# A two-phase FFN: up-projection in pairs of seven half products, all down blocks behind it, split squares kept in DRAM

## The chip, the cores and the metric

One core of a Trainium2 chip runs the whole kernel: three layers of a network on 1024 tokens, float32 throughout, one launch. The metric is device time in microseconds (us); each time given for the kernel before comes from three runs of it or from one profiled execution. The engines are named as in the profile: PE (TensorE matmul), DVE (VectorE), ACT (ScalarE), POOL (GpSimd), SP (SyncE, which issues DMAs).

## The reference, cut to what is touched

```
m = rmsnorm(h, g_mlp[i])                                             # [1024 tokens, 1024]
h = h + jnp.square(jax.nn.relu(m @ w_up[i])) @ w_down[i]             # 1024 -> 4096 -> 1024
gate = jax.nn.sigmoid(rmsnorm(h, g_ple[i]) @ w_ple_gate[i])
h = h + gate * (p[i] @ w_ple_proj[i])
return rmsnorm(h, g_final)
```

Everything ahead of these lines (a recurrent and latent-attention layer, a state-space layer, a convolution and attention layer) is the same in both kernels. The change concerns the second line, called the FFN below.

## The kernel before, in words

Float32 products run on PE as three matmuls: each operand is split into a high part (rounded to the PE's float32r) and a low part (what is left), and hi·hi, lo·hi and hi·lo are added in PSUM. One matmul takes 128 rows of weights and 512 tokens. Making a low part is a subtraction on DVE or POOL; making a high part is a copy on ACT or POOL.

Weights come as slabs of 512 KB. SP fetches them in the order of use into the two slots of `w_stage` (`fetch`, L614), each when the slab two earlier has been split (`s_w_ready`). POOL splits them into a ring of eight entries of `w_hi` and `w_lo`; an entry holds two 128-row tiles (`entry_hi` L707, `entry_lo` L711), and is free when PE has used it.

The order of the FFN is the list `FFN_ORDER`. A block is 512 of the 4096 hidden columns and has four up slabs (`up`, L1459) and four down slabs (`down`, L1485). Up slabs of block b+1 stand between the up and the down slabs of block b, so that while PE works on one kind, the other engines prepare the other. An up slab is 48 matmuls: 8 row tiles, 2 token halves, 3 parts. DVE then takes the relu and the root out of PSUM (`up_tile`, L2973), ACT squares it (L2176), and `upper_split` and `lower_split` (L2980 to L3001) with their ACT copies (L2184 to L2194) make what the down slabs read.

Seven of the eight down blocks use seven products of half size where a plain 2 x 2 product of quarters has eight (the list `SEVEN`, in the form that keeps sums of sums). Quarters of the weights are added on DVE (`weight_sums`, L3010 to L3015), quarters of the squares in the splits; each product goes to a half bank of PSUM, and DVE adds it where it belongs (`down_added`, L3032). A down slab is so 42 matmuls, not 48. The last block is plain (`last_down`, L1507).

## Time and profile before

| | us |
|---|---|
| median of 3 runs (2645.07 to 2648.64) | 2646.43 |
| the profiled execution, first to last instruction | 2643.2 |
| first matmul of the FFN (L1459) | 1876.5 |
| first matmul of the plain last block (L1507) | 2492.9 |
| PE busy over the span | 2572.9 (97%) |
| DVE, ACT, POOL busy over the span | 1599.2, 1001.6, 1140.9 |

The profile has one execution. Its busy PE counts a matmul from its start to its modelled end, and matmuls overlap, so the spacing of their starts is what they cost. A low busy share of DVE or POOL over the span says little of a stretch: rows further down are from stretches of the FFN alone. The profile gives no duration of the execution outside its first and last instruction; the median of the runs is 3.2 us above that span.

### The profile page before, as it was taken

What the parts mean: (1) busy time and instruction counts of PE and PEld (TensorE: products, weight loads), DVE (VectorE), ACT (ScalarE), POOL (GpSimd) and SP (SyncE); (2) the same over time, 40 slices, a digit from 0 to 9 for tenths busy, and PEclk for the clock granted to TensorE, in tenths of its full rate; (3) what the DMA queues carried; (4) which work ended last, traced back from release to release, by engine and by line L of the source; (5) the groups of instructions that cost most, each with busy time, mean ns of one, the idle gap of its engine ahead of it and who ended that gap; (6) DMA issues with size and microseconds to landing.
All of it is one profiled execution on the core that took longest, in us unless ns stands there. A gap on an engine that the chain in (4) does not pass through costs nothing.

```text
span 2643.2 us, 33209 instructions
## 1 busy us (share of the span) xinstructions
PE 2572.9 (97%) x12880; PEld 2055.9 (78%) x12880; DVE 1599.2 (61%) x1936; ACT 1001.6 (38%) x1434; POOL 1140.9 (43%) x1422
## 2 busy tenths in 40 slices
PE   8999999999999999999999999999999999999998
PEld 6877878687787787877776777767888888888886
DVE  6636663777647648557776455564455565555556
ACT  3527881436405315225365445563201111111132
POOL 4633344532432432432442222214565557655653
PEclk9999999999999999999999999999999999999999
DMA  3110002212112112111230010003111111111312
GB/s 139 48 51 27 24 25 90 86 59 100 52 55 73 58 49 71 66 59 66 90 112 24 25 33 25 33 17 104 56 49 48 48 56 56 54 43 49 120 47 80
DMA packets 44822, 156.36 MB, mean 59 GB/s; under 512 B 4928, under 2 KB 5312, under 8 KB 44672
## 3 DMA queue, kind: packets, MB, share of 16 engines
q1 hardware_dynamic: 31392, 110.11, 12.8%
q10 hardware_dynamic: 13280, 44.17, 4.6%
q8 instruction: 103, 1.69, 0.3%
q14 instruction: 47, 0.39, 0.0%
HBM read 141.55 MB, written 12.71 MB: 58 GB/s over the span
## 4 chain that ended last, share of the span: by engine, by line
PE 85%; DVE 8%; ACT 4%; issue 2%; POOL 1%; ACTq 0%; DVEq 0%; POOLq 0%
PE PS L784 38%; PE PS L1459 13%; PE PS L1485 10%; PE PS L1114 4%; PE PS L1021 3%; PE PS L1507 2%; PE PS L1347 1%; PE PS L920 1%; PE PS L1330 1%; PE PS L1147 1%; PE PS L1157 1%; PE PS L1151 1%; PE PS L934 1%; PE PS L1370 1%; DVE mla_neg_max L2397 1%
## 5 line engine op out<-in xcount | busy, mean ns | idle before, releaser
L637 POOL CAST w_hi<-w_stage 128x1024 fp32r<-128x1024 f32 x130 | 145.0, 1115 | 1048.4 <-PE PS L784 758.2
L640 POOL TENSOR_TENSOR w_lo<-w_stage,w_hi 128x256 fp32r<-128x256 f32 x520 | 492.9, 979 | 10.4
L784 PE MATMUL PS<-XH,w_hi 128*128 128x512 f32 x1216 | 386.7, 399 | 9.0 <-ACT ssd_z L1899 3.3
L784 PE MATMUL PS<-XL,w_hi 128*128 128x512 f32 x1216 | 375.9, 390 | 0.0
L784 PE MATMUL PS<-XH,w_lo 128*128 128x512 f32 x1216 | 375.4, 390 | 0.0
L784 PEld LDWEIGHTS PS<-XH,w_hi 128*128 128x128 f32 x1216 | 221.5, 188 | 65.4 <-issue 12.9
L784 PEld LDWEIGHTS PS<-XH,w_lo 128*128 128x128 f32 x1216 | 228.3, 188 | 48.7
L784 PEld LDWEIGHTS PS<-XL,w_hi 128*128 128x128 f32 x1216 | 228.3, 188 | 48.6
L711 POOL TENSOR_TENSOR w_lo<-w_stage,w_hi 128x256 fp32r<-128x256 f32 x260 | 220.1, 853 | 0.0
L707 POOL CAST w_hi<-w_stage 128x256 fp32r<-128x256 f32 x260 | 125.7, 486 | 185.6 <-PE PS L1459 108.2
L1459 PE MATMUL PS<-raw_hi,w_hi 128*128 128x512 f32 x512 | 158.2, 390 | 0.0
L1459 PE MATMUL PS<-raw_hi,w_lo 128*128 128x512 f32 x512 | 157.8, 389 | 0.0
L1459 PE MATMUL PS<-raw_lo,w_hi 128*128 128x512 f32 x512 | 157.7, 389 | 0.0
L1485 PE MATMUL PS<-ffn_u_hi,w_hi 128*128 128x512 f32 x392 | 152.6, 389 | 0.0
L1485 PE MATMUL PS<-ffn_u_hi,w_lo 128*128 128x512 f32 x392 | 152.6, 389 | 0.0
L1485 PE MATMUL PS<-ffn_u_lo,w_hi 128*128 128x512 f32 x392 | 152.6, 389 | 0.0
L3032 DVE TENSOR_TENSOR H<-H,PS 128x512 f32<-128x512 f32 x140 | 96.1, 686 | 76.9 <-PE PS L1485 76.9
L2973 DVE SCALAR_TENSOR_TENSOR ffn_t<-PS,root 128x1024 f32<-128x1024 f32 x32 | 39.2, 1225 | 154.2 <-PE PS L1459 145.0
L2176 ACT ACTIVATE ffn_t<-ffn_t 128x1024 f32<-128x1024 f32 x32 | 34.0, 1061 | 240.1 <-DVE ffn_t L2973 240.1
L1459 PEld LDWEIGHTS PS<-raw_hi,w_hi 128*128 128x128 f32 x512 | 96.1, 188 | 20.3 <-issue 0.5
L1459 PEld LDWEIGHTS PS<-raw_lo,w_hi 128*128 128x128 f32 x512 | 96.1, 188 | 19.9
L1459 PEld LDWEIGHTS PS<-raw_hi,w_lo 128*128 128x128 f32 x512 | 96.1, 188 | 19.9
(459 smaller groups left out, 5421.5 us busy)
## 6 DMA issues: line engine op xcount, KB each, us to landing
w_stage<-w SPq DMA_DIRECT2D x202, 512.0 KB, 3.4
ssd_sum_rows<-sums_kept ACTq DMA_DIRECT2D x32, 512.0 KB, 3.7
H<-x_t ACTq DMA_DIRECT2D x8, 512.0 KB, 8.3
pj_kept<-ple_proj_tiles ACTq DMA_DIRECT2D x8, 512.0 KB, 2.6
h_kept<-H ACTq DMA_DIRECT2D x8, 512.0 KB, 3.0
H<-h_kept ACTq DMA_DIRECT2D x4, 1024.0 KB, 5.5
out_t<-out_tiles SPq DMA_DIRECT2D x16, 256.0 KB, 2.1
x_again<-x_t ACTq DMA_DIRECT2D x12, 256.0 KB, 3.1
```

The source lines that it names most:

```text
L637: nc.gpsimd.tensor_copy(w_hi[:, slot, :, :], w_stage[:, slot, :, :]).then_inc(s_w_hi, 1)
L640: nc.gpsimd.tensor_tensor(w_lo[:, slot, k:k + 2, :], w_stage[:, slot, k:k + 2, :], w_hi[:, slot, k:k + 2, :].bitcast(F32), ALU.subtract).t ...
L707: nc.gpsimd.tensor_copy(ring(w_hi, e), src).then_inc(s_eh.sem, 1)
L711: nc.gpsimd.tensor_tensor(ring(w_lo, e), src, ring(w_hi, e).bitcast(F32), ALU.subtract).then_inc(done, count)
L784: mm = nc.tensor.matmul(outs[:, half, :], wt[:, slot, k, :], a[:, k - first, half * HB:(half + 1) * HB], start=(k == whole[0] and wt is w_ ...
L1021: mm = nc.tensor.matmul(PS[:, 2 * (n % 2) + half, :], wt[:, n % 2, k, :], a[:, k, half_cols(half)], start=(k == 0 and wt is w_hi and a is ...
L1114: mm = nc.tensor.matmul(PS[:, half, :], wt[:, n % 2, k, :], a[:, k, half * HB:(half + 1) * HB], start=(k == 0 and wt is w_hi and a is XH), ...
L1459: mm = nc.tensor.matmul(PS[:, 2 * (c % 2) + half, :], ring(wt, e + k // 2, k % 2), a[:, k, half * HB:(half + 1) * HB], start=(k == 0 and w ...
L1485: mm = nc.tensor.matmul(PS[:, BANK[j], :], ring(wt, e + i, k), a[:, ACTS_AT[j], k, :], start=(j not in BEFORE and k == 0 and wt is w_hi an ...
L1507: mm = nc.tensor.matmul(PS[:, 4 + 2 * e + half, :], ring(wt, e0 + k // 2, k % 2), a[:, t, half * HB:(half + 1) * HB], start=(first and wt ...
L2973: v.scalar_tensor_tensor(out=FT[:, c % 2, :], in0=flat(c % 2), scalar=0.0, in1=RSQ[:, :], op0=ALU.max, op1=ALU.mult).then_inc(s_ue, 1)
L3032: v.tensor_tensor(dst, dst, src, ALU.add).then_inc(s_dr, 1)
```

## The change

Up slabs are taken in pairs. Two pairs stay plain; for the other 14, a pair (1024 rows by 256 hidden columns by 1024 tokens) becomes seven products of quarters, each of 4 row tiles by 512 tokens by 3 parts, 12 matmuls. Sums of the token quarters are made once, before the phase (`token_sums`, `sums_lo`). Sums of weight quarters are made for each pair: three on DVE (`pair_sums`), one on POOL (`pair_difference`). ACT makes the high parts of all weights from here on (`pair_hi`, `down_hi`), POOL the low parts (`pair_part`, `down_part`).

All up pairs run first, then all down blocks. The split squares no longer stay in SBUF: for each pair seven pieces (four in the last two pairs), each 128 x 2 x 512 float32, are made in one of a few `U_PLACE`s, stored to DRAM by SP (`store`), and loaded again before their down block (`load`: four DMAs a block, of two pieces of both pairs each, the last of one).

The diff, cut to its core:

```diff
-FFN_ORDER = [("up", 0, 0), ("up", 0, 2), ("up", 0, 1), ("up", 0, 3)]
-for _b in range(1, FFN_BLOCKS):
-    FFN_ORDER += ([("up", _b, 0), ("up", _b, 2)] + [("down", _b - 1, _s) for _s in range(4)]
-                  + [("up", _b, 1), ("up", _b, 3)])
+PAIRS, PLAIN_PAIRS, DOWN_BLOCKS = 2 * FFN_BLOCKS, 2, FFN_BLOCKS - 1
+FFN_ORDER = [("up", _p // 2, _q) for _p in range(PAIRS) for _q in (_p % 2, _p % 2 + 2)]
+FFN_ORDER += [("down", _b, _s) for _b in range(DOWN_BLOCKS) for _s in range(4)]
 FFN_ORDER += [("last", FFN_BLOCKS - 1, _s) for _s in range(4)]
...
+            def next_slab(n):
+                sp.wait_ge(s_w_ready, 4 * (n - 1))
+                fetch(n, n % 2)
...
+            for p in range(PLAIN_PAIRS + 1, PAIRS):
+                stores(p - 2, slice(0, 2))
+                next_slab(pair_slab(p))
+                stores(p - 2, slice(2, 7))
+                next_slab(pair_slab(p) + 1)
+            p = PAIRS - 1
+            stores(p - 1, slice(0, 2))
+            next_slab(d0)
...
+            load(0, 0)
+            stores(p - 1, slice(2, 4))
...
+            load(0, 3)
+            next_slab(d0 + 1)
...
+            load(0, 1)
...
+            load(0, 2)
+            stores(p, slice(0, 2))
+            next_slab(d0 + 2)
+            stores(p, slice(2, 4))
...
+            for group in range(4):
+                load(1, group)
+            next_slab(d0 + 3)
+            for b in range(DOWN_BLOCKS - 1):
+                next_slab(d0 + 4 * b + 4)
+                next_slab(d0 + 4 * b + 5)
+                if b + 2 < DOWN_BLOCKS:
...
+                    for group in range(4):
+                        load(b + 2, group)
...
+                next_slab(d0 + 4 * b + 6)
+                next_slab(d0 + 4 * b + 7)
...
+            def up_pair(p):
+                for i, j in enumerate(SEVEN):
+                    if i in (4, 6):
+                        pe.wait_ge(s_w_ready, 4 * (n + 1 + (i == 6)))
+                    else:
+                        s_pd.wait(pe, 5 * turn + i + 1 - (i > 4))
...
+                    elif j in BEFORE:
+                        pe.wait_ge(s_ue, up_read({3: "c22", 4: "u3"}[j], p))
...
+                    for k in range(4):
+                        for wt, hl in ((w_hi, 0), (w_hi, 1), (w_lo, 0)):
+                            mm = nc.tensor.matmul(PS[:, 4 * (p % 2) + BANK[j], :], ring(wt, e + 2 * i + k // 2, k % 2), up_acts(j, hl, k),
...
+            for p in range(PLAIN_PAIRS, PAIRS):
+                if p > PLAIN_PAIRS:
+                    square_quad(p - 1, "f21")
+                u_hi(QUADS[p - 1][2], p - 1)
+                first_copied(p)
+                pair_hi(p, 4)
+                for j in QUADS[p - 1][3:]:
+                    u_hi(j, p - 1)
+                pair_hi(p, 5)
+                pair_hi(p, 6)
...
+            def pair_sums(p):
+                n, turn = pair_slab(p), p - PLAIN_PAIRS
+                a11, a12, a21, a22 = (w_stage[:, m, 4 * h:4 * h + 4, :] for m in range(2) for h in range(2))
+                for slot in range(2):
+                    dve.wait_ge(s_w_loaded[slot], 16 * (n // 2) + 16)
...
+                v.tensor_tensor(WS2[:, 0, :, :], a21, a22, ALU.add).then_inc(s_ws, 1)
+                dve.wait_ge(s_ws, 3 * turn + 1)
+                v.tensor_tensor(WS2[:, 1, :, :], WS2[:, 0, :, :], a11, ALU.subtract).then_inc(s_ws, 1)
...
+            for p in range(PLAIN_PAIRS, PAIRS):
+                u3(p)
+                c22(p)
+                f(3, p)
+                f(1, p)
+                if p + 1 < PAIRS:
+                    pair_sums(p + 1)
+                else:
+                    weight_sums(0, 0)
+                c12(p)
+                f(8, p)
+                u_steps(p, p + 1 if p + 1 < PAIRS else None)
```

On DVE `u_steps` makes the low parts of pieces 1 and 3, the last PSUM sum `c21` and its relu, the differences of pieces 5, 7, 6 and 4, and the other low parts. `SEVEN` is 1, 6, 5, 7, 2, 3, 4; of a pair's weights, products 1, 2 and 4 take a quarter as loaded, 6, 5 and 3 take DVE's sums, 7 takes POOL's difference. The second slab of a pair holds two of the quarters that the first sum adds.

Three places show the order that this makes.

SP before, from the program's start to its end (`w_stage` are the weight slots; the branch rows are the loop over slabs):

```order
L614 DMA w_stage_49<-w 128x1024 x2
L620 UNCONDITIONAL_BRANCH
L620 ISA
L614 ISA
L614 DMA w_stage_49<-w 128x1024
L614 ISA
L614 DMA w_stage_49<-w 128x1024
L620 REGISTER_ALU
L620 COMPARE_AND_BRANCH
L628 DMA out_t<-out_tiles_165 128x512 x16
```

SP after, between two second slabs of pairs in the middle of the up phase (the first and last row are such fetches; `ffn_u_place0` to `4` are the places of split squares, `u_kept` is in DRAM):

```order
L715 DMA w_stage_49<-w 128x1024
L737 DMA u_kept<-ffn_u_place0_161 128x1024
L737 DMA u_kept<-ffn_u_place1_162 128x1024
L715 DMA w_stage_49<-w 128x1024
L737 DMA u_kept<-ffn_u_place2_163 128x1024
L737 DMA u_kept<-ffn_u_place3_164 128x1024
L737 DMA u_kept<-ffn_u_place0_161 128x1024
L737 DMA u_kept<-ffn_u_place4_165 128x1024
L737 DMA u_kept<-ffn_u_place1_162 128x1024
L715 DMA w_stage_49<-w 128x1024
```

Before, only weights stood in this queue until the outputs. Now two stores stand ahead of the first slab's fetch of each pair, and five between it and the second slab's.

DVE before, from one up tile to the first PSUM add of the down slabs:

```order
L2973 SCALAR_TENSOR_TENSOR ffn_t<-PS,root 128x1024
L3010 TENSOR_TENSOR w_sums<-w_stage 128x256
L3012 TENSOR_TENSOR w_sums<-w_sums,w_stage 128x256
L3013 TENSOR_TENSOR w_sums<-w_stage 128x256
L3015 TENSOR_TENSOR w_sums<-w_stage,w_sums 128x256
L2973 SCALAR_TENSOR_TENSOR ffn_t<-PS,root 128x1024
L3032 TENSOR_TENSOR ffn_shared<-ffn_shared,PS 128x512
```

DVE after, from the weight sums of the next pair to the first difference (`up_w_sums` are those sums, `up_partial` the running sum of products, `ffn_t` the quarters that become squares):

```order
L3421 TENSOR_TENSOR up_w_sums<-w_stage 128x512
L3423 TENSOR_TENSOR up_w_sums<-up_w_sums,w_stage 128x512
L3425 TENSOR_TENSOR up_w_sums<-w_stage,up_w_sums 128x512
L3367 TENSOR_TENSOR ffn_t<-up_partial,PS 128x512
L3381 SCALAR_TENSOR_TENSOR ffn_t<-ffn_t,root 128x512
L3409 TENSOR_TENSOR ffn_u_place_165<-ffn_t,ffn_u_place_165 128x512
L3409 TENSOR_TENSOR ffn_u_place_161<-ffn_t,ffn_u_place_161 128x512
L3371 TENSOR_TENSOR ffn_t<-up_partial,PS 128x512
L3381 SCALAR_TENSOR_TENSOR ffn_t<-ffn_t,root 128x512
L3402 TENSOR_TENSOR ffn_u_place_162<-ffn_t 128x512
```

Before, the weight sums belonged to down slabs alone. Now the three sums of the next pair stand ahead of the rest of this pair's evacuation and split.

SP after, at the turn from the up phase to the down phase (`u_last_kept` takes the pieces of the plain last block, `ffn_u_even` and `ffn_u_odd` are the loaded pieces of even and odd blocks; the weight fetches are the second, the third, and the fourth to sixth down slab):

```order
L764 DMA ffn_u_even_last_172<-u_kept 128x2048
L715 DMA w_stage_49<-w 128x1024
L764 DMA ffn_u_even_171<-u_kept 128x2x2048 x2
L737 DMA u_last_kept<-ffn_u_place0_161 128x1024
L737 DMA u_last_kept<-ffn_u_place1_162 128x1024
L715 DMA w_stage_49<-w 128x1024
L737 DMA u_last_kept<-ffn_u_place2_163 128x1024
L737 DMA u_last_kept<-ffn_u_place3_164 128x1024
L764 DMA ffn_u_odd_173<-u_kept 128x2x2048 x3
L764 DMA ffn_u_odd_173<-u_kept 128x2048
L715 DMA w_stage_49<-w 128x1024 x3
```

Before, the squares of the first down block were already in SBUF when its slabs came. Now seven megabytes a block stand in the same queue as the weights, the second block's ahead of the fourth down slab.

## Rows read from the trace of the kernel before

**Rows 1.** The chain that ended last, from the FFN on: start, length, what.
```profile
1943.67 38.08 PE PS L1485 x168
1981.75 43.52 PE PS L1459 x192
...
2471.34 21.76 PE PS L1459 x96
2493.11 10.88 PE PS L1507 x48
```

**Rows 2.** Busy time of the engines in the blocks, then PE clock, DMA share, GB/s.
```profile
1943.50:2470.70 527.20, 527.20 (x2327) 436.68 (x2326) 300.23 (x436) 72.79 (x85) 335.98 (x583) 1.00 0.17 53
```

**Rows 3.** Timeline of DVE, a split right behind a down block: start, length, instruction.
```profile
2144.98 0.69 DVE L3032 TENSOR_TENSOR H<-H,PS 128x512 f32<-128x512 f32 x1 [0.67 <-PE PS L1485]
2145.59 1.07 DVE L2980 TENSOR_TENSOR ffn_u_sums<-ffn_t 128x512 f32<-128x512 f32 x1
...
2153.60 0.88 DVE L3001 TENSOR_TENSOR ffn_u_lo<-ffn_u_sums,ffn_u_hi 128x512 fp32r<-128x512 f32 x1
```

**Rows 4.** Timeline of DVE, the lower half of a later split.
```profile
2169.09 0.69 DVE L2989 TENSOR_TENSOR ffn_u_sums<-ffn_t 128x512 f32<-128x512 f32 x1 [1.13 <-ACT ffn_t L2176]
...
2173.50 0.68 DVE L3001 TENSOR_TENSOR ffn_u_lo<-ffn_u_sums,ffn_u_hi 128x512 fp32r<-128x512 f32 x1
```

**Rows 5.** Timeline of POOL, inside the stretch of rows 3.
```profile
2150.89 1.71 POOL L711 TENSOR_TENSOR w_lo<-w_stage,w_hi 128x256 fp32r<-128x256 f32 x1
```

**Rows 6.** Groups of instructions by form, FFN blocks alone: busy us, mean ns.
```profile
L711 POOL TENSOR_TENSOR w_lo<-w_stage,w_hi 128x256 fp32r<-128x256 f32 x183 | 149.7, 824 | 0.0
...
L711 POOL TENSOR_TENSOR w_lo<-w_sums,w_hi 128x256 fp32r<-128x256 f32 x108 | 79.6, 737 | 0.0
...
L3015 DVE TENSOR_TENSOR w_sums<-w_stage,w_sums 128x256 f32<-128x256 f32 x27 | 16.7, 620 | 0.0
...
L3012 DVE TENSOR_TENSOR w_sums<-w_sums,w_stage 128x256 f32<-128x256 f32 x27 | 11.5, 425 | 0.9
...
L2184 ACT ACTIVATE ffn_u_hi<-ffn_t 128x512 fp32r<-128x512 f32 x12 | 7.6, 634 | 215.1 <-PE PS L1485 214.6
```

**Rows 7.** The same view of the whole span, one group of POOL.
```profile
L654 POOL TENSOR_TENSOR mla_q_lo<-mla_q,mla_q_hi 128x1024 fp32r<-128x1024 f32 x8 | 19.0, 2378 | 78.7 <-ACT mla_q_hi L1664 78.7
```

**Rows 8.** DMA issues: KB each, median us from issue to landing.
```profile
w_stage<-w SPq DMA_DIRECT2D x202, 512.0 KB, 3.4
...
pj_kept<-ple_proj_tiles ACTq DMA_DIRECT2D x8, 512.0 KB, 2.6
```

**Rows 9.** Timeline of ACT, copies that wait for 512 KB loads issued in a row.
```profile
13.57 1.06 ACT L1580 ACTIVATE XH<-H 128x1024 fp32r<-128x1024 f32 x1 [0.54 <-DMA H<-x_t]
14.85 1.06 ACT L1580 ACTIVATE XH<-H 128x1024 fp32r<-128x1024 f32 x1 [0.22 <-DMA H<-x_t]
16.12 1.06 ACT L1580 ACTIVATE XH<-H 128x1024 fp32r<-128x1024 f32 x1 [0.22 <-DMA H<-x_t]
```

**Rows 10.** Busy time while two loads of 2 MB ran; the last two columns are DMA.
```profile
2475.00:2477.00 2.00, 2.00 (x10) 1.65 (x9) 2.00 (x4) 0.00 (x0) 0.83 (x2) 1.00 1.00 410
...
2479.00:2481.00 2.00, 2.00 (x11) 1.65 (x10) 0.99 (x2) 0.00 (x0) 1.37 (x2) 1.00 1.04 420
```

More of the change, by code:

```diff
@@ L199, with pair_slab, _uses @@
 FFN_ORDER += [("last", FFN_BLOCKS - 1, _s) for _s in range(4)]
 FFN_AT = {_key: N_FFN + _n for _n, _key in enumerate(FFN_ORDER)}
+def pair_slab(p):
+    return N_FFN + 2 * p
 RING = 8
-ENTRY, ENTRY_OWNER, FREED = {}, [], {}
+ENTRY, USED, FREED = {}, [], {}
 _freed = 0
-for _key in FFN_ORDER:
-    if _key[0] == "last":
-        break
-    _n, _size = FFN_AT[_key], 4 if _key[0] == "up" else 7
-    ENTRY[_n], FREED[_n] = len(ENTRY_OWNER), _freed
-    ENTRY_OWNER += [(_n, _i if _i < _size - 1 else None) for _i in range(_size)]
-    _freed += _size - 1
+def _uses(n, parts, slabs, wide):
+    global _freed
+    ENTRY[n], FREED[n] = len(USED), _freed
+    for _i in range(parts):
+        if _i in slabs:
+            USED.extend([("slab", slabs[_i])] * wide)
+        else:
+            _freed += 1
+            USED.extend([("part", _freed)] * wide)
@@ new lines, in stores, with stored, used @@
+            def stores(p, part):
+                for j in [j for j, q in LOWS if q == p][part]:
+                    store(j, p)
+            def stored(p):
+                n = sum(len(QUADS[q]) for q in range(p))
+                for r in range(U_PLACES):
+                    if PLACE_ORDER[:n].count(r):
+                        s_us[r].wait(sp, 16 * PLACE_ORDER[:n].count(r))
+            def used(token):
+                if token[0] == "slab":
+                    sp.wait_ge(s_slab, token[1])
+                else:
+                    s_we.wait(sp, token[1])
@@ new lines, in load @@
+            def load(b, group):
+                first, last = 2 * group, min(2 * group + 2, 7)
+                if b >= 2:
+                    n = FFN_AT["down", b - 2, 3]
+                    used(USED[ENTRY[n] + last - 1])
+                if b % 2:
+                    dst = U_ODD[:, first:last, :, :, :]
+                else:
+                    dst = U_EVEN[:, first:last, :, :, :] if group < 3 else U_EVEN4[:, :, :, :].unsqueeze(1)
+                sp.dma_start(dst.rearrange("p q i l t -> p q (i l t)").bitcast(F32),
+                             u_kept[b, first:last, :, :, :, :].rearrange("q p i l t -> p q (i l t)")).then_inc(s_ur[b % 2][group].sem, 16)
@@ L624, in _ @@
+            for n in range(N_PLE - 4, NSLAB):
+                next_slab(n)
             for half in range(2):
@@ L753, in program @@
+            for d in range(4 * DOWN_BLOCKS):
+                for i in range(7):
+                    down_part(d, i)
+            for turn, n in enumerate(range(N_PLE - 4, NSLAB)):
+                plain_slab(n, 2 * PLAIN_PAIRS + turn)
         class Tiles:
@@ new lines, in first_copied, with used @@
+            def first_copied(p):
+                turn = p - PLAIN_PAIRS
+                kind, count = pair_use(p, 0)
+                s_we.wait(act, count)
+                if turn:
+                    act.wait_ge(s_ue, up_read("c21", p - 1))
+                nc.scalar.activation(U2[:, :], PS[:, 4 * (p % 2) + BANK[1], :], ACT.Copy).then_inc(s_p1.sem, 1)
+            def used(token):
+                kind, count = token
+                if kind == "slab":
+                    act.wait_ge(s_slab, count)
+                else:
+                    s_we.wait(act, count)
@@ new lines, in ring, with pair_hi @@
+            def ring(t, e, wide=1):
+                return t[:, :, :, :].rearrange("p a b c -> p (a b) c")[:, e % RING * 2:e % RING * 2 + 2 * wide, :]
+            def pair_hi(p, i):
+                j, n = SEVEN[i], pair_slab(p)
+                e, turn = ENTRY[n] + 2 * i, p - PLAIN_PAIRS
+                used(USED[e + 1 - RING])
+                if j in PAIR_RAW:
+                    slot, k = PAIR_RAW[j]
+                    act.wait_ge(s_w_loaded[slot], 16 * (n // 2) + 16)
+                    src = w_stage[:, slot, k:k + 4, :]
+                else:
+                    if j == 7:
+                        s_w3.wait(act, turn + 1)
+                    else:
+                        act.wait_ge(s_ws, 3 * turn + {5: 1, 6: 2, 3: 3}[j])
+                    src = WS2[:, SUM_AT[j], :, :]
+                nc.scalar.activation(ring(w_hi, e, 2), src, ACT.Copy).then_inc(s_ah.sem, 1)
```

736 lines of the change are left out of this document (499 added, 237 removed).

## The prediction

> **What bounds the kernel now.** I read the chain of waits in order of time first, from the FFN on. It is PE and nothing else: 38.08 us for the 168 matmuls of four down slabs, 43.52 us for the 192 of four up slabs, in turn, without a wait between [rows 1]. Both give 0.2267 us per matmul. Then the busy times of that stretch [rows 2]: PE is busy for all of its 527.2 us at a granted clock of 1.00 (the 2.4 GHz level), DVE for 57% of it, POOL for 64%, ACT for 14%, and DMA for a 0.17 share. So a matmul that is taken away here shortens the kernel by 0.2267 us, as long as the other engines and the queue keep up. The other three views say how much they have left: timelines of DVE and POOL where both work at once [rows 3 to 5], groups by form [rows 6, 7], and the DMA views [rows 8 to 10].
>
> **What is removed.** A plain pair is 96 matmuls, 21.76 us; seven half products are 84, 19.04 us. Over 14 pairs that is 168 matmuls, **-38.1 us**. The down slabs (42) and the plain last block keep theirs. A half product is 12 matmuls, 2.72 us in an up pair and 1.36 us in a down slab.
>
> **What must fit under 19.04 us.** ACT gets 19 operations of 128 x 512 a pair at 0.63 us [rows 6], 12 us: it fits. POOL gets seven low parts and a difference of 128 x 512. No row has that form; between 0.737 us for 256 columns and 2.378 us for 1024 [rows 6, 7] it is 1.28 us alone, 10.3 us a pair. DVE gets 23 operations. Behind a down block nine splits of 11 times 512 columns took from 2145.59 to 2154.48 us [rows 3], 0.81 us per 512 columns, with POOL at work beside them (a low part took 1.71 us there [rows 5], against 0.74 alone); with POOL mostly waiting, eight took from 2169.09 to 2174.18 us [rows 4], 0.64 us. DVE reads PSUM beside POOL undisturbed: 0.61 us from start to start [rows 3]. So 17 operations with two SBUF operands and 6 with one from PSUM take 14.5 to 17.4 us. Each engine fits by itself. What doesn't is a loop through all of them and the queue.
>
> **The loop.** Per pair SP now issues two weight fetches and seven stores of 512 KB. Nine transfers at 1.27 us, the spacing at which loads issued in a row landed (14.85 to 16.12 [rows 9]), are 11.4 us, also what 410 to 420 GB/s make of them [rows 10]. It is their order that counts. Say the second slab of pair p+1 has landed at W.
> - DVE runs in order: three weight sums, two evacuation steps, two low parts, two more steps, the first difference of pair p. Eight have two SBUF operands (0.81 us; POOL has its difference and three low parts to do meanwhile), two read PSUM (0.61 us): 7.7 us.
> - ACT copies the difference, then the first product out of PSUM, then makes the high part of pair p+1's fifth product: 3 x 0.63 = 1.9 us. It can't take the last of these first, since it stands behind the copy that waits.
> - POOL makes that product's low part: 1.4 us (1.28 with the 824 to 737 ns of rows 6). Only this frees the slot for the next pair's first slab.
> - SP fetches it: 3.4 us to landing [rows 8]. Five stores of pair p and the second slab's fetch follow: 6 x 1.27 = 7.6 us, since their pieces are ready (DVE makes them within 6.5 us of the difference) before their turn in the queue.
> - Five hand-overs of 0.04 us, as between dependent operations of one engine: 0.2 us.
>
> That is W of the next pair: **22.2 us**, more than 19.04 and more than 21.76. From below: DVE at 0.64 us throughout, POOL at 1.28, is 20.7 us. From above: if POOL's four operations (5.1 us) each held DVE up in full, 26 us. I take 22.2, for the stretch of rows 3 is the nearest, and keep 20.7 to 24.5 for the range.
>
> PE sees it as a wait for the second product (sums, high part, low part: W + 3.8 us). Pair 3's second slab comes by the same steps some 20 us into pair 2, which costs 2.5 us. Twelve turns from pair 3 to pair 15 cost 12 x (22.2 - 19.04) = 37.9 us. **Up phase: -38.1 + 2.5 + 37.9 = +2.3 us.** The time saved in matmuls is waited for again.
>
> **The turn to the down phase.** A load of two pieces is 2 MB, 5.1 us of the queue. Count from W of pair 15. Its last matmul ends at 3.8 + 6 x 2.72 = 20.1. The first down slab's fetch goes out at 11.0 (the loop's steps, with a square on ACT in place of DVE's difference) and lands at 14.4; behind it stand 2 MB (19.5), two stores (22.0), 1 MB (24.6), a slab (25.8), 2 MB (30.9), 2 MB (36.0). PE wants the third product's pieces at 22.8 and gets them at 30.9 (8.1 us), the fifth's at 33.6 and gets them at 36.0 (2.4 us). The fourth down slab is fetched behind four stores, a slab and the 7 MB of the second block: 36.0 + 6.4 + 17.8 + 1.2 = 61.4. DVE's sums for it stand in order ahead of the third slab's adds, and PE's sixth product there, due at 56.4, waits for one: 61.4 + 1.9 (sums, 425 and 620 ns [rows 6]) + 1.2 = 64.5, 8.1 us. **+18.6 us**, between 10 (fetches that partly pass the loads) and 25.
>
> **Each later block.** The loads for the block after next start when the last slab's second product is done, 2.7 us into it; 2.1 us later data flows, 17.8 us long, then the third slab of the next block: 24.1 us, 14.5 into that block. DVE stands at its sums from 11.7 and adds again from 16.4; PE's sixth product is due at 16.3 and starts at 17.6: 1.3 us, five times, **+6.5 us**, from 0 to 12.
>
> **Nothing elsewhere.** Token sums (16 DVE operations, about 11 us, before the first evacuation) hide behind two plain slabs; PSUM is used twice as deep; the tail keeps its order.
>
> Sum: 2.3 + 18.6 + 6.5 = +27.4 us on the profiled span of 2643.2 us. The median of the runs is 3.2 us above that; 2646.4 + 27.4 = **2674 us**.
>
> **The rivals.**
> - *The second slab doesn't wait for the stores: faster.* If its fetch overtook them (the rows show a full queue in order for loads, and nothing of stores beside loads), the loop would be 22.2 - 5 x 1.27 = 15.9 us, and PE would set the pace at 19.04. Left are 12 us at the turn and 3 behind it: -38.1 + 15 = -23 us, 2623 us. The point that decides is 19.04 us a pair. For it: a lone store lands in 2.6 us [rows 8], and DMA was at 0.17 [rows 2]. Against: 1.27 us at 1.00 share is all that the queue gave. Chance 0.2.
> - *DVE and POOL in each other's way.* With the loop at 24.5 to 26 us: 12 x 5.5 to 7 = 66 to 84 us, so 2702 to 2720 us. For it: 1.71 us against 0.74 [rows 5]. Against: DVE's own 0.81 was only a quarter above 0.64. Chance 0.1. The Trainium skill (SBUF — State Buffer, "Who interferes with whom") has it that a DVE operation with two SBUF inputs and a POOL operation that reads SBUF exclude each other for a whole instruction. By that the loop would be the 26 us. Rows 3 and 5 agree as to POOL and bear out only part of it for DVE.
> - *All of it even.* The loop at its low bound (1.7 x 12 = 20 us) and the turn at 10, with 5 behind: -38.1 + 2.5 + 35 = about -1 us, 2646 us. Chance 0.1.
>
> **How the numbers follow.** The forecast has 0.6. The low ends of its terms (2.5 + 20 + 10 + 0 - 38.1) give -6, the high ends (2.5 + 65.5 + 22 + 10 - 38.1) +62. From 2630 to 2712 us leaves out most of the first rival and the top of the second, about 2 in 10. A change of 0.2% (5.3 us) is about what runs of this kernel can tell from none. Faster: the first rival and a little of the forecast's low end, 0.22. Same: the even case, 0.1. Slower: 0.68.
>
> **What would show it.** PE waiting at the second product of most pairs, for POOL's low part, that for DVE's sums, that for the fetch of `w_stage`; starts of up pairs 22 us apart; fetches with a median far over 3.4 us to landing, and the second slab landing behind stores; one or two waits of 8 us in the first down block and its fourth slab. It is wrong if pairs start 19.04 us apart, or if PE waits at the sixth product, for the PSUM sums on DVE, rather than at the second. If stores go out while a fetch issued later lands first, the first rival holds.

## The result, and the profile after

The changed kernel takes 2752.09 us (median of 4 runs, 2747.81 to 2755.55), the kernel before, beside it, 2645.75 us (2645.03 to 2648.64): a ratio of 1.0398, 95% interval 1.0383 to 1.0413. The forecast had the direction right and the size wrong: +27 us was forecast, +106 us came, outside the range. The profiled execution spans 2752.3 us.

The busy times of the up pairs and of the down blocks, with the columns of [rows 2] (length; PE, PEld, DVE, ACT, POOL; PE clock, DMA share, GB/s):

```profile
1924.90:2283.70 358.80, 301.36 (x1176) 238.43 (x1176) 295.46 (x321) 152.30 (x270) 176.13 (x114) 0.91 0.50 184
2285.80:2602.30 316.50, 284.43 (x1176) 231.46 (x1177) 179.41 (x305) 77.11 (x193) 148.38 (x205) 0.93 0.60 235
```

In [rows 2] PE was busy for the whole stretch at a clock of 1.00. Now it is 361.8 us from the last plain matmul (1921.9) to the end of the 14 pairs (2283.7), where plain ones took 14 x 21.76 = 304.6: **+57.2 us** (forecast +2.3). From there to the end of the split down blocks it is 318.6 us, where seven blocks of [rows 1] took 266.6: **+52.0 us** (forecast 18.6 + 6.5 = +25.1). Together that is 109.2 us, the difference of the two profiled spans (2752.3 and 2643.2): the rest of the kernel is as before. Each of the two stretches has 1176 matmuls, 266.6 us at 0.2267. The windows above leave out 3.0 and 2.0 us of waiting ahead of them; with these PE idles for 60.4 us in the up phase and 34.1 in the down blocks, and its own work is 34.8 and 17.8 us longer than it would be at full clock.

What PE waits for there (waits of PE; us in total, times, longest):

```profile
PE PS L1700 <- DVE ffn_t L3363: 53.1, 13, 4.2
PE PS L1723 <- POOL w_lo L944: 27.5, 8, 8.6
PE PS L1723 <- DMA ffn_u_even<-u_kept: 6.6, 1, 6.6
...
PE PS L1700 <- DVE ffn_t L3309: 3.4, 1, 3.4
```

L3363 is the second PSUM sum of a pair, so PE waits at the sixth product, once a pair, for 4.2 us: the sign that the forecast named for being wrong. The pace, from DVE's first weight sum of each pair (view of one line: duration min/median/max in ns, first and last start):

```profile
L3421 DVE TENSOR_TENSOR up_w_sums<-w_stage x12: 691/693/694, 1951.1 to 2235.6; 128x512 f32<-128x512 f32 x12
```

Eleven pairs in 284.5 us: **25.9 us a pair**, where 22.2 was forecast and a plain pair took 21.76. The chain of waits through one such pair, then POOL and DVE near its end:

```profile
2003.07 0.70 DVE up_w_sums L3421
...
2003.79 1.67 DVE up_w_sums L3423
...
2008.10 3.40 DVE ffn_u_place L3409 x2
...
2018.27 4.04 DVE ffn_u_place L3409 x3
...
2022.33 0.32 SPq L737
...
2022.70 2.33 DMA w_stage<-w
2025.02 3.54 issue
2028.56 0.70 DVE up_w_sums L3421
```

```profile
2020.05 3.38 POOL L932 TENSOR_TENSOR w_lo<-w_stage,w_hi 128x512 fp32r<-128x512 f32 x2
...
2028.61 1.78 POOL L917 TENSOR_TENSOR up_w_sums<-w_stage 128x512 f32<-128x512 f32 x1 [5.18 <-DMA w_stage<-w]
```

```profile
2022.23 0.68 DVE L3358 TENSOR_TENSOR ffn_t<-up_partial,PS 128x512 f32<-128x512 f32 x1
```

It is a loop, and a loop through the second slab's fetch, as forecast; but it closes elsewhere. DVE works from the sums to its last low part of a square piece (2003.07 to 2022.3: 19.2 us); SP, in order, issues the last store (L737) and only then the fetch, at 2022.70. The slab has landed 5.8 us later, behind the stores: POOL, which does nothing else then, waits for it until 2028.5. The place that this slab goes to had come free only at 2021.7, with the seventh product's low part, the first of the two at 2020.05. The DVE instructions themselves are long. Their groups by form from 1950 to 2200 us (busy us, mean ns), then one of POOL's:

```profile
L3409 DVE TENSOR_TENSOR ffn_u_place<-ffn_u_place 128x512 fp32r<-128x512 f32 x39 | 46.3, 1205 | 0.0
L3409 DVE TENSOR_TENSOR ffn_u_place<-ffn_t,ffn_u_place 128x512 fp32r<-128x512 f32 x30 | 41.6, 1411 | 0.0
...
L3402 DVE TENSOR_TENSOR ffn_u_place<-ffn_t,ffn_u_place 128x512 f32<-128x512 f32 x10 | 17.5, 1750 | 0.2 <-DMA u_kept<-ffn_u_place 0.2
L3423 DVE TENSOR_TENSOR up_w_sums<-up_w_sums,w_stage 128x512 f32<-128x512 f32 x10 | 16.6, 1663 | 0.3
...
L3425 DVE TENSOR_TENSOR up_w_sums<-w_stage,up_w_sums 128x512 f32<-128x512 f32 x10 | 6.9, 692 | 0.3
```

```profile
L917 POOL TENSOR_TENSOR up_w_sums<-w_stage 128x512 f32<-128x512 f32 x10 | 17.9, 1788 | 55.0 <-DMA w_stage<-w 55.0
```

The same form on DVE takes 692 ns (L3425) or 1663 ns (L3423). The sum that is long, L3423, is the one beside which POOL makes the pair's difference (L917). L3358, which adds a PSUM bank to one operand in SBUF, takes 0.68 us although POOL makes a low part at the same time (the rows of 2020.05 and 2022.23).

In the down blocks, the third slab of a block, followed in the one case (timelines of SP, DVE and PE):

```profile
2383.33 7.13 SPq L764 DMA_DIRECT2D ffn_u_odd<-u_kept  x4
2390.50 9.48 SPq L715 DMA_DIRECT2D w_stage<-w  x2
```

```profile
2404.72 0.42 DVE L3437 TENSOR_TENSOR w_sums<-w_stage 128x256 f32<-128x256 f32 x1 [3.01 <-DMA w_stage<-w]
...
2405.52 0.96 DVE L3440 TENSOR_TENSOR w_sums<-w_stage 128x256 f32<-128x256 f32 x1
...
2407.87 2.06 DVE L3459 TENSOR_TENSOR H<-H,PS 128x512 f32<-128x512 f32 x3
```

```profile
2285.82 1.08 PE L1723 MATMUL PS<-ffn_u_even,w_hi 128*128 128x512 f32 x2 [2.01 <-POOL w_lo L944]
...
2408.69 1.07 PE L1723 MATMUL PS<-ffn_u_even,w_hi 128*128 128x512 f32 x2 [2.27 <-POOL w_lo L944]
```

The fetch goes out behind four loads, lands 14.2 us later, DVE stands for 3.0 us, and PE waits 2.27 us (the row of PE ahead of that one is the first wait of the turn). The profile names POOL's low part, but the sixth product, at which PE stands here, also waits for DVE's add of the third, the first of the three at 2407.87: it ended 0.1 us before PE went on, and the low parts of this slab had been made by 2399.6. The DMA issues, to [rows 8]:

```profile
w_stage<-w SPq DMA_DIRECT2D x202, 512.0 KB, 3.4
```

Over the whole kernel the fetches' median is the 3.4 us it was, where the forecast expected far more: what is late is shown by the single fetches above, not by the median. The clock, in three windows from one wait of the up phase on (columns as above):

```profile
2019.70:2023.80 4.10, 0.00 (x0) 0.00 (x0) 3.96 (x5) 0.63 (x1) 3.73 (x3) 0.92 1.04 422
2023.84:2029.95 6.11, 6.11 (x14) 4.75 (x15) 2.54 (x4) 2.38 (x4) 1.34 (x1) 0.50 0.62 245
2030.20:2045.00 14.80, 14.80 (x67) 12.23 (x66) 14.01 (x17) 7.78 (x14) 7.22 (x6) 1.00 0.28 92
```

PE does nothing for 4.1 us, and the next 14 matmuls take 6.11 us at a granted clock of 0.50, the 1.2 GHz level, in place of 3.2; then it is at 1.00 again.

### The profile page after: what moved, and what is told of

The parts are those of the page before. It is cut to its first block, busy times and chain, and to the rows that moved or that the text cites. A ratio compares the mean times of both kernels' runs of the same rounds, so it can differ in the third digit from the quotient of the medians.

```text
span 2752.3 us, 33519 instructions
## 1 busy us (share of the span) xinstructions
PE 2587.9 (94%) x12712; PEld 2052.3 (75%) x12712; DVE 1783.9 (65%) x2126; ACT 1156.7 (42%) x1810; POOL 1122.2 (41%) x1116
## 4 chain that ended last, share of the span: by engine, by line
PE 66%; DVE 16%; DMA 6%; ACT 6%; issue 5%; POOL 1%; ACTq 0%; SPq 0%; DVEq 0%; POOLq 0%
PE PS L994 36%; PE PS L1723 6%; DMA w_stage<-w 5%; DVE ffn_u_place L3409 4%; PE PS L1324 4%; PE PS L1231 2%; PE PS L1745 2%; PE PS L1700 1%; PE PS L1557 1%; PE PS L1130 1%; PE PS L1540 1%; PE PS L1357 1%; PE PS L1367 1%; PE PS L1361 1%; PE PS L1144 1%
## 5 line engine op out<-in xcount | busy, mean ns | idle before, releaser
L831 POOL TENSOR_TENSOR w_lo<-w_stage,w_hi 128x256 fp32r<-128x256 f32 x520 | 494.2, 982 | 10.4
L1700 PE MATMUL PS<-ffn_raw,w_hi 128*128 128x512 f32 x336 | 125.4, 459 | 58.7 <-DVE ffn_t L3363 53.1
L1723 PE MATMUL PS<-ffn_u_even,w_hi 128*128 128x512 f32 x384 | 125.0, 408 | 24.9 <-POOL w_lo L944 18.3
L1700 PE MATMUL PS<-ffn_token_sums,w_hi 128*128 128x512 f32 x448 | 140.0, 394 | 1.7 <-POOL w_lo L932 1.7
L1723 PE MATMUL PS<-ffn_u_odd,w_hi 128*128 128x512 f32 x336 | 107.2, 401 | 9.2 <-POOL w_lo L944 9.2
L2099 ACT ACTIVATE ssd_x<-ssd_conv 128x1024 f32<-128x1024 f32 x16 | 16.9, 1060 | 227.2 <-DVE ssd_conv L2927 227.2
L944 POOL TENSOR_TENSOR w_lo<-w_sums,w_hi 128x256 fp32r<-128x256 f32 x112 | 83.3, 764 | 60.8 <-ACT w_hi L2494 60.8
L944 POOL TENSOR_TENSOR w_lo<-w_stage,w_hi 128x256 fp32r<-128x256 f32 x84 | 63.3, 754 | 108.8 <-ACT w_hi L2494 108.8
L1723 PEld LDWEIGHTS PS<-ffn_u_even,w_hi 128*128 128x128 f32 x384 | 75.3, 198 | 43.2 <-POOL w_lo L944 20.2
L932 POOL TENSOR_TENSOR w_lo<-up_w_sums,w_hi 128x512 fp32r<-128x512 f32 x56 | 87.1, 1566 | 49.0 <-ACT w_hi L2482 47.6
L1700 PEld LDWEIGHTS PS<-ffn_token_sums,w_hi 128*128 128x128 f32 x448 | 85.3, 191 | 21.6 <-POOL w_lo L932 3.3
L2927 DVE SCALAR_TENSOR_TENSOR ssd_conv<-PS,VC,ssd_conv 128x1023 f32<-128x1023 f32 (+2 forms) x72 | 92.3, 1282 | 2.6
## 6 DMA issues: line engine op xcount, KB each, us to landing
ffn_u_even<-u_kept SPq DMA_DIRECT2D x12, 2048.0 KB, 10.3
```

The source lines that it names most:

```text
L831: nc.gpsimd.tensor_tensor(w_lo[:, slot, k:k + 2, :], w_stage[:, slot, k:k + 2, :], w_hi[:, slot, k:k + 2, :].bitcast(F32), ALU.subtract).t ...
L932: nc.gpsimd.tensor_tensor(ring(w_lo, e, 2), src, ring(w_hi, e, 2).bitcast(F32), ALU.subtract).then_inc(done, count)
L944: nc.gpsimd.tensor_tensor(ring(w_lo, e), src, ring(w_hi, e).bitcast(F32), ALU.subtract).then_inc(done, count)
L1700: mm = nc.tensor.matmul(PS[:, 4 * (p % 2) + BANK[j], :], ring(wt, e + 2 * i + k // 2, k % 2), up_acts(j, hl, k), start=(j not in BEFORE an ...
L1723: mm = nc.tensor.matmul(PS[:, 4 * (d % 2) + BANK[j], :], ring(wt, e + i, k), down_acts(b, j, k, hl), start=(j not in BEFORE and k == 0 and ...
L2927: ins = v.scalar_tensor_tensor(out=y[:, d:TOK], in0=src[:, 0:TOK - d], scalar=wcol(3 - d), in1=y[:, d:TOK], op0=ALU.mult, op1=ALU.add)
```

## The experiments

**Three edits, apart and together.** The first changes SP's order alone:

```diff
                 next_slab(pair_slab(p))
-                stores(p - 2, slice(2, 7))
                 next_slab(pair_slab(p) + 1)
+                stores(p - 2, slice(2, 7))
```

> Only SP's order in the up phase changes: the second slab of a pair is fetched before the five stores of the pair two back, not after them. Theory A (a loop through DVE and the queue): in the pair from 2003 us DVE is at work from its sums (2003.07) to its last evacuation step (2025.02) without a gap, and the second slab, whose fetch was issued at 2022.70 behind the last store, lands at 2028.5. POOL's last low part there ends near 2021.7, so the fetch now goes out some 1 us earlier and with less ahead of it and lands near 2025.5: a pair takes 22.5 to 23 us in place of 25.9, 12 times 3 us, so about 2716 us (2705 to 2724). Theory B (the queue alone holds the loop, DVE's stretch follows from it): the loop falls to the 15.9 us of the forecast's first rival, PE sets the pace at 19.04, 12 times 6.8, so about 2670 us or less. Theory C (PE's lower clock after its waits sets the pace): no change, 2752 us.

Measured: 2713.0 us (2708.8 to 2719.0), 1.0262 times the kernel before (1.0243 to 1.0280). The first sums of 14 pairs:

```profile
L3421 DVE TENSOR_TENSOR up_w_sums<-w_stage x14: 691/693/695, 1927.6 to 2224.7; 128x512 f32<-128x512 f32 x14
```

22.85 us a pair, 3 us less, as theory A had it. The queue's order is 39 us of the 106. Theories B and C fall. It isn't the whole loop, which still takes longer than a plain pair's 21.76. One pair of this kernel (the profile's chain, then DVE's timeline):

```profile
2034.60 1.72 POOL w_lo L932
...
2036.33 3.24 DMA w_stage<-w
```

```profile
2040.46 0.69 DVE L3421 TENSOR_TENSOR up_w_sums<-w_stage 128x512 f32<-128x512 f32 x1 [0.89 <-issue]
```

The fetch now goes out as soon as the seventh low part has freed its place (2036.3), 18.8 us behind the pair's first sum (2017.49; 18.7 in the changed kernel), and the next sums start 4.1 us later. DVE still stands for 0.9 us ahead of them: the loop is DVE, ACT and POOL up to that low part, then the fetch. Of the 3 us, 1.0 was SP's wait for the last store's data (2021.7 to 2022.70), and most of the rest the transfers ahead of the fetch (5.8 us from issue to landing, about 4 now).

The second edit moves four of POOL's eight operations of a pair to DVE:

```diff
+                v.tensor_tensor(WS2[:, 2, :, :], a11, a21, ALU.subtract).then_inc(s_ws, 1)
...
+            def pair_lo(p, i):
...
+                v.tensor_tensor(lo, src, hi.bitcast(F32), ALU.subtract).then_inc(s_w3.sem, 1)
...
-                pair_part(p, 0)
-                pair_difference(p)
-                for i in range(1, 7):
+                for i in (1, 2, 4, 6):
                     pair_part(p, i)
```

> The pair's difference and three of its seven low parts (first, fourth and sixth product) are made by DVE in place of POOL; SP's order is that of the changed kernel. DVE so gets four more operations with two SBUF operands a pair, POOL four fewer of 1.33 to 1.79 us. Theory A (a DVE operation with two SBUF operands and a POOL operation exclude each other for a whole instruction): in the pair from 2003 us the stretched DVE operations took 7.5 us more than their 0.68 or so, for eight POOL operations, 0.94 us each; four fewer give back 3.75 us and four more at 0.65 us cost 2.6 us, so a pair takes about 1.1 us less, 12 times, 2739 us (2725 to 2748), and the DVE operations beside no POOL operation read 0.68 or 0.69 us. Rival (DVE's operations are long for a reason of their own, such as the transfers into SBUF): four more operations cost 2.6 us a pair or more, 12 times, 2783 us.

Measured: 2740.6 us (2739.7 to 2745.3), 1.0368 (1.0351 to 1.0386). DVE got more to do, and the loop got shorter. Two groups of DVE by form, from 1950 to 2200 us, and the pace:

```profile
L3402 DVE TENSOR_TENSOR ffn_u_place<-ffn_t,ffn_u_place 128x512 f32<-128x512 f32 x10 | 17.9, 1790 | 0.0
...
L3423 DVE TENSOR_TENSOR up_w_sums<-up_w_sums,w_stage 128x512 f32<-128x512 f32 x10 | 6.9, 692 | 0.3
```

```profile
L3421 DVE TENSOR_TENSOR up_w_sums<-w_stage x14: 691/693/695, 1930.0 to 2251.9; 128x512 f32<-128x512 f32 x14
```

L3423, its POOL neighbour gone, falls from 1663 to 692 ns; L3402, beside which POOL still makes the fifth product's low part, stays long (1750, now 1790). A pair takes 24.76 us, 1.1 us less, the number that exclusion gives; a DVE slow of itself would have given 28.5.

The third edit changes SP's order from the turn on:

```diff
...
-                    for group in range(4):
-                        load(b + 2, group)
+                    load(b + 2, 0)
+                    load(b + 2, 1)
+                    next_slab(d0 + 4 * b + 6)
+                    load(b + 2, 2)
+                    load(b + 2, 3)
...
```

> Only SP's order from the turn on changes: in each down block the third slab's fetch goes between the second and third load of the block after next; at the turn two stores go behind the slab fetch, and the fourth down slab goes between the loads of the second block. Theory A (PE waits there for DVE, DVE for a slab that stands behind 7 MB of loads): the third slab lands some 16 us after the start of the fourth slab of the block before, in place of 24, so DVE has its sums in time and PE's waits of 2.2 to 4.0 us in the later blocks go, with the stretches at the lower clock behind them (19 and 12 us in all), and of the 18.4 us of waits at the turn some 8 to 10 go: about 2712 us (2700 to 2727). Rival (in the down phase DVE and POOL hold each other up so that PE would wait anyway): within 5 us of 2752. The up phase is untouched.

Measured: 2721.7 us (2720.0 to 2723.8), 1.0289 (1.0272 to 1.0307). PE's waits of the down blocks:

```profile
PE PS L1729 <- DMA ffn_u_even<-u_kept: 9.9, 1, 9.9
...
PE PS L1729 <- POOL w_lo L950: 2.5, 2, 1.8
```

34.1 us of waits became 12.4. What stays is 10.6 us at the turn, most of it one wait for the first block's data, longer than it was (9.9 in place of 6.6), and 1.8 us in the last split block; of the turn's waits less went than expected (6.6 us for 8 to 10). The three together:

> The three edits together: the second slab's fetch first, four of POOL's operations of a pair on DVE, loads and fetches mixed from the turn on. Theory A: the loop of a pair is then DVE's own work, 21.95 us less 1.1, about 20.8 us, with the fetch just inside it: 12 times 5.1 us from the up phase and 36 to 40 us from the turn and the blocks, 2752 - 61 - 38 = 2653 us (2635 to 2675). Should DVE's work come below 19.04 us, PE sets the pace: 12 times 6.9 us and some of the first pair's wait, 2628 us. If the edits hit the same time (the queue alone), the sum is less than that of the three apart: over 2680 us.

Measured: 2670.9 us (2666.1 to 2673.5), 1.0096 (1.0079 to 1.0112). 81 us of the 106 are explained by three edits, in the range of theory A but at its upper end. A pair took 21.7 us, not 20.8, and in the one looked at (from 2064.7 us) DVE had no gap; and the first pair waited for 12.6 us, since two low parts of DVE stood beside POOL's splits of the token sums (DVE's timeline, then PE's wait):

```profile
1907.98 10.10 DVE L3415 TENSOR_TENSOR ffn_u_place<-ffn_t,ffn_u_place 128x512 fp32r<-128x512 f32 x2
```

```profile
PE PS L1698 <- DVE w_lo L3309: 12.6, 1, 12.6
```

**POOL out of the up phase.** Two kernels build on the three edits. In the first the token sums' splits go to DVE too; in the second POOL does nothing between the plain pairs and the down slabs, and DVE's operations are laid so that few stand directly behind the one they depend on:

```diff
...
-            for i, tq in enumerate((1, 2)):
-                s_th.wait(pool, 3 + i)
...
+            sums_lo(7, 3)
+            sums_lo(4, 4)
+            pair_lo(PLAIN_PAIRS, 0)
             pair_sums(PLAIN_PAIRS)
-            pair_lo(PLAIN_PAIRS, 0)
```

> On top of the three edits together: the two low parts of the token sums that POOL makes (128 x 2048, 11.67 us for both, beside which two low parts of DVE took 10.10 us) go to DVE, the first weight low part goes ahead of DVE's weight sums, and at the turn the loads are asked for in the order in which PE wants them. Theory A: the first pair's wait of 12.98 us shrinks to about 4, since the squares of the first pair are split, stored and their places freed some 7 us earlier; the turn's 8.94 us shrinks to about 5. 2671 - 9 - 4 = 2658 us (2650 to 2665). Rival (the first pair waits for the stores' own time, not for DVE behind POOL): only the turn gains, 2667 us.

Measured: 2659.5 us (2658.1 to 2659.8), 1.0052 (1.0035 to 1.0068), in the range. The first pair waited for 3.7 us, as expected; the turn for 7.2 us, more than the 5 expected.

```diff
...
-            for p in range(PLAIN_PAIRS, PAIRS):
-                pair_part(p, 0)
-                pair_difference(p)
-                for i in range(1, 7):
-                    pair_part(p, i)
...
                 u3(p)
+                pair_lo(p + 1, 0)
                 c22(p)
-                f(3, p)
                 f(1, p)
...
```

> As the run with the new start, and POOL does nothing between the plain pairs and the down slabs: DVE makes all seven low parts and the sums, with hardly an operation directly behind the one it depends on, and two stores go ahead of the second slab, three behind it. DVE then has 31 operations a pair. Theory A (the lock is what stretched them): alone they take 0.60 to 0.65 us, 18.8 to 20.2 us in place of 21.64 for 27; a pair takes 19.04 (PE) to 20.2 us: 2658 - 12 x 2.1 = 2633 us (2624 to 2642), the first below the kernel before. Rival (DVE's operations are long of themselves, 21.64 / 27 = 0.80 us each): 31 take 24.8 us, 2658 + 12 x 3.1 = 2695 us.

Measured: 2649.8 us (2646.0 to 2654.7), 1.0014 (1.0005 to 1.0024). The mechanism held, the number did not: 9.7 us came, where 25 were forecast (2624 to 2642). DVE by form from 1950 to 2200 us, two of its largest groups:

```profile
L3396 DVE TENSOR_TENSOR ffn_u_place<-ffn_u_place 128x512 fp32r<-128x512 f32 x48 | 33.4, 696 | 0.0
...
L3396 DVE TENSOR_TENSOR ffn_u_place<-ffn_t,ffn_u_place 128x512 fp32r<-128x512 f32 x36 | 24.8, 690 | 0.0
```

No group is over 0.70 us; operations start 0.60 us apart. The low parts of the square pieces, 1205 and 1411 ns in the changed kernel, are the same instructions on the same tiles. But the pair took 20.65 us (19.04 to 20.2 was expected), for DVE had a new wait ahead of its sums, for the second slab:

```profile
2089.49 0.69 DVE L3413 TENSOR_TENSOR up_w_sums<-w_stage 128x512 f32<-128x512 f32 x1 [2.14 <-issue]
```

**Down to PE's pace.** Five more kernels took that loop in hand. The first makes the sixth and seventh products' high and low parts earlier, on DVE (ahead of four splits) and on ACT:

```diff
                 pair_hi(p, 4)
-                for j in QUADS[p - 1][3:]:
-                    u_hi(j, p - 1)
+                late = QUADS[p - 1][3:]
+                u_hi(late[0], p - 1)
                 pair_hi(p, 5)
+                for j in late[1:2]:
+                    u_hi(j, p - 1)
                 pair_hi(p, 6)
+                for j in late[2:]:
+                    u_hi(j, p - 1)
...
```

> The kernel in which POOL does nothing in the up phase, with the operations that free the second slab put earlier: ACT makes the high parts of the sixth and seventh products between its copies of the square pieces, DVE makes their low parts ahead of four splits, and one store, not two, stands ahead of the second slab's fetch. Theory A: a pair there takes 20.6 us, 18.6 of DVE's work and some 2 us in which DVE waits for the second slab; the fetch now goes out 1.9 us earlier, the loop falls to 18.7 us, below PE's 19.04, so a pair takes 19.04 to 19.3 us: 2650 - 12 x 1.4 = 2633 us (2629 to 2638). Rival (DVE's waits only move, to a high part that ACT now makes later): 20.6 us a pair as before, 2650 us.

Measured: 2638.1 us (2635.6 to 2640.6), 0.9968 (0.9956 to 0.9981): below the kernel before, at the upper edge of the range. A pair took 19.9 us, where 19.04 to 19.3 was expected. The second adds three small edits to it, two of them here:

```diff
+            pair_lo(PLAIN_PAIRS, 1)
+            pair_lo(PLAIN_PAIRS, 2)
+            sums_lo(7, 3)
+            sums_lo(4, 4)
...
             load(1, 0)
-            load(1, 1)
             next_slab(d0 + 3)
+            load(1, 1)
...
```

> The same, and three small waits besides: the first pair's second and third low parts go ahead of the two splits of the token sums (PE waited 4.03 us for them), the fourth down slab goes behind one load of 2 MB in place of two, and the third slab of the last split block goes ahead of the 4 MB for the last block (waits of 2.21 and 2.14 us). Theory A: 2633 - 4 - 2 - 2 = 2625 us (2620 to 2631), 0.8% below the kernel before. Rival (what is gained at one place is waited for at the next, as in the changed kernel): 2633 us, or 2650 us if the loop didn't get shorter.

Measured: 2641.7 us (2637.0 to 2644.6), 0.9983 (0.9974 to 0.9992). The rival held: what the first pair gained at its second product it lost at its sixth (a wait of 3.2 us for 0.4), for the two splits now stood ahead of DVE's evacuations there, and the second block's first slab, fetched behind loads of that block, came later, so that the sixth product of the slab before it waited 3.3 us for 1.2. The third again starts from the first of the five:

```diff
...
-                stores(p - 2, slice(2, 3))
                 next_slab(pair_slab(p) + 1)
-                stores(p - 2, slice(3, 7))
+                stores(p - 2, slice(2, 7))
...
```

> As the run with the tighter loop, whose pair still took 19.9 us: 18.7 of DVE's work and some 1.1 us before the first sum, where it waited for the second slab behind the first one and a store. Here all five stores go behind the second slab's fetch, and one evacuation step goes ahead of the first sum. Theory A: the slab lands 1.27 us earlier, the loop falls to 18.7 us and PE sets the pace at 19.04: 2638 - 12 x 0.85 = 2628 us (2624 to 2632). Rival (the pieces' places are now freed too late, ACT waits for the stores and DVE behind it): 19.9 us or more, 2638 us or slower.

Measured: 2636.4 us (2633.0 to 2639.5), 0.9967 (0.9955 to 0.9979); a miss, hardly faster than the first of the five. The fourth builds on it; of its edits, the one at the turn:

```diff
...
-            stores(p - 1, slice(3, 4))
-            stores(p, slice(0, 2))
...
+            for group in range(1, 4):
+                load(1, group)
+            stores(p - 1, slice(3, 4))
+            stores(p, slice(0, 4))
...
```

> The same, with the first pair's token-sum splits put where DVE waits anyway (one in its 2.66 us wait for a store, one behind the last plain evacuation), and from the turn on the five stores that only the last block needs go behind the 14 MB of the first two blocks, the third slab of the last split block ahead of the last block's 4 MB. Theory A: the first pair's 4.1 us falls to about 1, the waits of the turn and the blocks (10.4 us and 2.1 at the lower clock) to about 6: 2628 - 3 - 6 = 2619 us (2614 to 2626). Rival (the queue moves 18 MB between pair 15 and the second block, 45 us at 1.27 us per 512 KB, and the order only moves the wait): 2625 us.

Measured: 2635.8 us (2631.7 to 2638.7), 0.9964 (0.9951 to 0.9978). The rival's mechanism held again; its waits of the down blocks:

```profile
PE PS L1697 <- POOL w_lo L926: 8.7, 2, 5.5
...
PE PS L1697 <- DMA ffn_u_even<-u_kept: 1.8, 1, 1.8
```

10.5 us in three waits, in the kernel before it 9.6 in six: the order moves the wait. Why the loop hadn't got down to 19.04 us shows in DVE's timeline (two pairs of this kernel):

```profile
2091.86 0.69 DVE L3292 TENSOR_TENSOR w_lo<-w_stage,w_hi 128x512 fp32r<-128x512 f32 x1 [0.84 <-ACT w_hi L2453]
...
2111.56 0.69 DVE L3292 TENSOR_TENSOR w_lo<-w_stage,w_hi 128x512 fp32r<-128x512 f32 x1 [0.85 <-ACT w_hi L2453]
```

The wait for the slab is gone, and DVE now waits for the seventh product's high part, whose place in the ring PE's third product frees; 19.70 us a pair. So the fifth kernel is the third with one split moved into that wait, and with the third slab of the last split block ahead of the last block's load:

```diff
...
                     pair_lo(following, 5)
-                    pair_lo(following, 6)
                 u_lo(7, p)
+                if following:
+                    pair_lo(following, 6)
                 u_lo(2, p)
```

> As the run with the stores behind the second slab, whose pair took 19.70 us: DVE waited 0.84 us for the seventh product's high part (its place in the ring comes free with PE's third product), and PE then 0.55 us at the sixth product. One split of a square piece is moved into that wait, and the third slab of the last split block goes ahead of the last block's 4 MB (2.06 us). Theory A (the loop is now PE to the ring to DVE and back, and one operation of 0.6 us fills the wait): a pair takes 19.04 to 19.1 us, 12 x 0.6 = 7 us, and 2 us of the last split block: 2636 - 9 = 2627 us (2623 to 2632). Rival (the wait is set elsewhere and the low part only comes later): 2634 to 2640 us.

Measured: **2626.5 us** (2626.2 to 2631.2), **0.9934** (0.9921 to 0.9948): 0.7% below the kernel before, and clear of it. Its pace, its busy times (columns as above) and what PE still waits for in the down blocks:

```profile
L3349 DVE TENSOR_TENSOR ffn_t<-up_partial,PS x14: 671/679/686, 1942.0 to 2190.7; 128x512 f32<-128x512 f32 x14
```

```profile
1924.60:2198.70 274.10, 270.43 (x1179) 221.02 (x1177) 260.71 (x430) 148.59 (x268) 1.66 (x3) 0.99 0.66 243
2198.70:2476.20 277.50, 269.41 (x1177) 221.54 (x1176) 177.30 (x309) 78.76 (x197) 148.44 (x206) 0.99 0.68 266
```

```profile
PE PS L1699 <- POOL w_lo L928: 6.5, 4, 3.2
...
PE PS L1699 <- DMA ffn_u_even<-u_kept: 1.6, 1, 1.6
```

A pair takes 19.13 us, PE's 19.04 but for 0.1. The up phase is 304.6 - 274.1 = 30.5 us below plain pairs, the down blocks 277.5 - 266.6 = 10.9 us above theirs.

## Why the prediction was wrong, point by point

- **What is removed** (-38.1 us) was right: the last kernel gets 30.5 of it in the up phase. Of the other 7.6 us, 3.7 are PE's idle time, one wait in the first pair, and 3.8 its own work above 266.6 us, at a granted clock of 0.99.
- **The loop** was right as a mechanism (DVE, then the fetch behind the stores, and PE waits once a pair) and mis-sized: 25.9 us for 22.2, 12 x 3.7 = 44 of the 55 us by which the up phase was off. The step that failed is "Eight have two SBUF operands (0.81 us ...)": DVE reached the end of its first difference 10.3 us after the first sum, not 7.7. With it fell the branch that was taken: the forecast followed DVE to its first difference and the fifth product's slot. In fact DVE's whole work up to the last store stood ahead of the fetch, 19.2 us. "Their pieces are ready before their turn in the queue" was wrong: the forecast has the last one ready 14.2 us after the first sum, it was ready after 19.2, and SP waits for it. One term was missing: the second slab's own place, which its fetch needs, comes free only with the seventh low part, 18.7 us after the first sum. Moving the stores behind the fetch gave 39 us; how much of that is SP's wait and how much the bytes ahead is read from one pair of each kernel (about 1 and 2 us), not run apart.
- **Why 0.81 was too little.** It was an average over nine splits beside few POOL operations. The kernel before has, in the stretch of [rows 3, 5], besides the one of rows 5:

```profile
2145.37 1.88 POOL L711 TENSOR_TENSOR w_lo<-w_stage,w_hi 128x256 fp32r<-128x256 f32 x2
...
2153.90 1.18 POOL L711 TENSOR_TENSOR w_lo<-w_stage,w_hi 128x256 fp32r<-128x256 f32 x1
```

  That is four low parts of 256 columns, one begun before the splits and one ended behind them. The splits took 1.85 us more than eleven times the 0.64 of [rows 4], which is two and a half low parts at 0.74. So the rows fitted a DVE that stands still while POOL works; the average hid it. In a pair eight POOL operations of 512 columns (1.33 us where nothing is beside them, 10.6 us) stand against 17 of DVE. The step should have charged DVE for POOL's time, not taken a mean. The full sum is the upper end: in the pair followed above DVE's long instructions together took 7.0 us more than at 0.69 us each.
- **The second rival** was this mechanism, with 2702 to 2720 us and a chance of 0.1; its loop of 24.5 to 26 us was right, in part by luck, since it has neither the wait for the last store nor the place of the second slab; and "DVE's own 0.81 was only a quarter above 0.64" was the wrong reason to doubt it. The Trainium skill (SBUF — State Buffer, "Who interferes with whom") says that a DVE instruction with two SBUF inputs and a GpSimd instruction that reads SBUF exclude each other for a whole instruction, and that a DVE instruction with at most one SBUF input, outside its two-port modes, is free of it. The runs agree: L3423 took 1663 ns beside POOL and 692 without, and L3358, with PSUM as one of its two sources, 0.68 us beside POOL.
- **The turn** was right in sum, 17.2 us of waits for 18.6, and in two of its terms: 6.6 us at the third product (8.1 forecast) and 8.6 at the third slab's sixth (8.1). That the sum is so near is partly luck: the 2.4 us at the fifth product didn't come, and 2.0 us at the very first product weren't in the forecast.
- **Each later block** was right as a mechanism and mis-sized: six waits of 1.8 to 3.6 us, each at the sixth product of a block's second slab, 16.9 us in all, for five of 1.3. In the one block followed above the fetch landed when the forecast said, 21.4 us after the loads began; DVE's four sums took 2.55 us for 1.9, two of them 0.96 and 0.94 beside POOL where the others took 0.42, and the rest lies behind them. The other blocks weren't followed one by one. The third edit took five of the six waits away; the one of 1.8 us in the last split block stayed.
- **The clock** was not in the forecast at all. In the down blocks, where PE is the bound, it is 17.8 us on top. In the up phase it is 34.8 us of PE's time that another wait would have filled: a pair's 19.04 and 2.9 are still under 25.9. That is argued, not run by itself.
- **The first rival** (fetches overtake stores) fell: the slab landed behind the stores, 5.8 us after its issue. Even put ahead of them by the first edit it gave a loop of 22.85 us, not 15.9, since its place comes free only after 18.8.

In sum: +55 us of error in the up phase (44 the loop, 9 ahead of it at the first pairs, where one wait of 3.4 us was for the last plain evacuation, the rest at the last pair), +27 in the down blocks (9 of waits, 18 of clock).

Open: the 7.8 to 10.5 us of waits that stay at the turn and in the blocks of the last five kernels. From pair 15 to the second block the queue moves some 18 MB (14 MB of loads, four slabs, four or five stores), and none of the three orders of it that these kernels have brought the sum lower; fewer bytes, or stores on another queue, weren't tried.

## What to carry to other kernels

Where DVE and POOL both work densely on SBUF, add POOL's time to that of DVE's two-SBUF-operand work as an upper bound (here 7 of POOL's 10.6 us a pair came on top); don't take DVE at an average from a stretch where POOL was sparse, and where POOL needs 1.33 us for what DVE does in 0.60, giving it all to DVE can be faster. For each fetch ask three things: what frees its place, what the issuing engine waits for ahead of it, and what bytes are ahead. Here the place came free 18.7 us into the loop, a store that waited for its data held the fetch back by another 1.0, and the stores ahead of it made its landing late. And a wait taken away from such a loop showed up at the next place: the fetch, then the second slab, then the seventh product's high part, until PE itself was the loop.
